# Sample attention of a hybrid decoder step: high and low parts as stationary columns, and four steps moved

## What is computed

```
h = RMSNorm(x);  z = h @ w_in          # 544 rows, one combined projection
A: mLSTM, 4 heads;  B: dilated sliding-window attention, 6 heads;  C: block-sparse attention, 6 heads
y = sum_b sigmoid(gate_b) * (branch_b @ w_br_b);  x = x + y @ w_out;  x = x + SwiGLU(RMSNorm(x))
def dsa_group_sample(q, k, v, buf, bias_tab, win, dil):      # B for the samples
    kv = concatenate([buf, stack([k, v])])                   # window buffer of 128 or 256 cached positions
    s = einsum('bthd,btjhd->bthj', q, g[:, :, :, 0]) * Dh ** -0.5 + bias
    p, lse = softmax_lse(s);  o = einsum('bthj,btjhd->bthd', p, g[:, :, :, 1])
```

## Time and profile before

| | |
|---|---|
| median of 3 runs | 998.3 us (997.5 to 999.62) |
| the profiled execution | 997.17 us |
| its span, first to last instruction | 995.4 us |
| TensorE matmul busy | 972.5 us, 98% |
| VectorE busy | 487.0 us, 49% |
| ScalarE busy | 337.5 us, 34% |
| granted TensorE clock, mean | 0.998 of full |

### The profile page before, as it was taken

One profiled execution on the slowest core, in us unless ns is written; L12 is line 12 of the kernel. 1 busy time (PEld: TensorE's weight loads), 2 busy tenths in 40 slices (PEclk: granted clock), 3 DMA queues, 4 the chain that ended last, 5 costly groups with the idle time before them and its releaser, 6 DMA issues.

```text
span 995.4 us, 18277 instructions
## 1 busy us (share of the span) xinstructions
PE 972.5 (98%) x7624; PEld 947.2 (95%) x7624; DVE 487.0 (49%) x886; ACT 337.5 (34%) x577; POOL 75.6 (8%) x106
## 2 busy tenths in 40 slices
PE   6999999999999999999999999999999999999998
PEld 5899989999889899999999999999999999999997
DVE  5735566444886122645355565555445555323232
ACT  7443233444553441322222342222222222222122
POOL 0100022011301100111113000000000000000000
PEclk9999999999999999999999999999999999999999
DMA  7586437322321764222222222222223222222302
GB/s 251 149 251 235 76 90 152 114 81 78 103 60 35 224 196 114 84 86 86 85 86 85 86 85 86 85 86 88 94 96 98 94 85 75 86 74 76 116 2 90
DMA packets 104909, 105.03 MB, mean 106 GB/s; under 512 B 11130, under 2 KB 101752, under 8 KB 104492
## 3 DMA queue, kind: packets, MB, share of 16 engines
q1 hardware_dynamic: 101224, 92.78, 30.3%
q0 software_dynamic: 3552, 11.08, 3.6%
q10 hardware_dynamic: 52, 0.01, 0.0%
HBM read 98.00 MB, written 15.45 MB: 114 GB/s over the span
## 4 chain that ended last, share of the span: by engine, by line
PE 89%; DVE 5%; issue 1%; ACT 1%; POOL 1%; SPq 1%; DMA 1%; ACTq 0%; DVEq 0%; POOLq 0%
PE acc L451 75%; PE acc L1108 2%; PE acc L1057 1%; PE acc L1033 1%; PE acc L1144 1%; POOL mt L830 1%; DVE w_lo L435 1%; PE acc L1091 1%; PE acc L911 1%; PE acc L900 1%; SPq L681 1%; PE acc L871 1%; PE acc L1017 1%; DVE h_lo L2069 1%; PE acc L1232 1%
## 5 line engine op out<-in xcount | busy, mean ns | idle before, releaser
L451 PE MATMUL acc<-h_hi,w_hi 128*128 128x256 f32 (+1 forms) x1520 | 465.1, 306 | 2.1 <-DVE w_lo L435 1.6
L451 PE MATMUL acc<-h_lo,w_hi 128*128 128x256 f32 (+1 forms) x1520 | 437.7, 288 | 0.0
L451 PE MATMUL acc<-h_hi,w_lo 128*128 128x256 f32 (+1 forms) x1520 | 435.8, 287 | 0.0
L451 PEld LDWEIGHTS acc<-h_hi,w_hi 128*128 128x128 f32 x1520 | 285.8, 188 | 10.3 <-issue 4.2
L430 ACT ACTIVATE w_hi<-raw 128x1024 fp32r<-128x1024 f32 x135 | 141.4, 1047 | 441.7 <-PE acc L451 441.6
L451 PEld LDWEIGHTS acc<-h_lo,w_hi 128*128 128x128 f32 x1520 | 286.1, 188 | 4.8 <-issue 2.4
L451 PEld LDWEIGHTS acc<-h_hi,w_lo 128*128 128x128 f32 x1520 | 286.1, 188 | 0.0
L435 DVE TENSOR_TENSOR w_lo<-raw,w_hi 128x1024 fp32r<-128x1024 f32 x135 | 165.3, 1225 | 112.5 <-ACT w_hi L430 107.8
L451 PE MATMUL acc<-s_hi,w_hi 128*128 128x256 f32 (+1 forms) x352 | 101.6, 288 | 0.0
L451 PE MATMUL acc<-s_lo,w_hi 128*128 128x256 f32 (+1 forms) x352 | 101.3, 288 | 0.0
L451 PE MATMUL acc<-s_hi,w_lo 128*128 128x256 f32 (+1 forms) x352 | 100.7, 286 | 0.0
(11 more groups left out here) (334 smaller groups left out, 1116.9 us busy)
## 6 DMA issues: line engine op xcount, KB each, us to landing
raw<-in_w_in SPq DMA_DIRECT2D x25, 1024.0 KB, 5.1
raw<-in_w_gate_up SPq DMA_DIRECT2D x22, 1024.0 KB, 4.9
raw<-in_w_down SPq DMA_DIRECT2D x8, 1024.0 KB, 4.8
rev<-tab POOLq DMA_DIRECT2D x1, 4352.0 KB, 19.1
ring<-in_cache_dsa_kv SPq DMA_DIRECT2D x4, 1024.0 KB, 6.7
raw<-in_w_out SPq DMA_DIRECT2D x4, 1024.0 KB, 4.7
out<-in_cache_dsa_kv SPq DMA_DIRECT2D x2, 2016.0 KB
ring<-in_cache_moba_k SPq DMA_DIRECT2D x48, 64.0 KB, 2.1
```

The lines of the kernel that those rows point to most:

```text
L451: ins = nc.tensor.matmul(acc[:, bank, 0:HALF[half]], a[:, k, :], two(b[:, kx + k, :], half), start=first and k == k0 and c == 0, stop=last ...
```

## The change

1. **Sample attention, keys.** `Qpad` is fp32r: columns 0 to 63 of a sample hold the high part of the queries, columns 64 to 127 the low part. The transposed keys are split: ScalarE writes the high part of four tiles (512 columns) into `KTs[n % 2]`, VectorE the low part. 22 steps take the place of 48. For each sample there are two fp32r passes (keys high, keys low) with the same stationary operand, in place of one fp32 matmul. The results of the high and the low queries stand in different partitions; ScalarE copies the other half (`low_s`) and VectorE adds (`sums`, three times).
2. **Values.** The same: `V_hi` (ScalarE, 1024 columns, two buffers) and `V_lo` (VectorE, in place of the ring's data) for each of the 11 steps, two fp32r passes of 128 columns for each sample; the new tokens' part comes last; the output is copied in two pieces, transposed in six tiles, and high and low are added (L2059's place).
3. **Block 0** has 64 high and 64 low columns in one stationary operand, and two passes in place of three.
4. **Moved:** `split_hi(0)` and `split_lo(0)` ahead of x's; ScalarE's exp and log of the mLSTM behind `split_hi(3)`; `factors` by a quarter of a block; the cache copies to blocks 66, 70 and 74; the end: sums of squares of the first seven slices and the first transposes ahead of the wait for the last slice. Due times of the sample attention are new.

```diff
-        Qpad = m("Qpad", [P, 2, NB, P])
+        Qpad = m("Qpad", [P, 2, NB, P], F32R)
...
-        KTs = Map(a_s + 8192, 2048)("KTs", [P, 2, 256])
+        V_hi = [Map(a_a + 9216, 4096)("V_hi0", [P, NB, P], F32R), Map(sq_at, 4096)("V_hi1", [P, NB, P], F32R)]
...
+        KTs = [Map(a_a + 9216, 4096)("KTs0", [P, 2, 512], F32R), Map(sq_at, 4096)("KTs1", [P, 2, 512], F32R)]
...
-        loads.append(([(0, 0, rows(w_in, 0, KD, 1024, 32)), (0, 32, rows(w_in, 0, KD, 1028, 96))], P))
+        loads.append(([(0, 0, rows(w_in, 0, KD, 1024, 32)), (0, 32, rows(w_in, 0, KD, 1028, 32))], P))
...
+                passes = ((hi, x_hi), (hi, x_lo)) if w == 0 else ((hi, x_hi), (hi, x_lo), (lo, x_hi))
...
-        T_SA, T_F = 33, 29.1
-        T_QK, D_QK = 1.3, 0.042
-        T_SM, T_P, D_PV = 3.4, 4.6, 0.05
+        T_SA, T_F = 33, 29.35
+        T_QK, D_QK = 1.3, 0.075
+        T_SM, T_P, D_PV = 2.95, 4.05, 0.11
...
+        k_steps = [(m, range(b, b + 4 // NC4[q])) for m, q in enumerate(Q_ORDER) for b in range(0, NB, 4 // NC4[q])]
+        k_ends = [max(n for n, step in enumerate(k_steps) if step[0] == m) + 1 for m in range(6)]
+        K_BANK = (2, 6, 7)
...
-                    when = (0.4, 0.41, 0.42, 0.43, 1.7, 2.05, 2.35, 2.7, 3.05, 3.4, 4.8, 4.9)
+                    when = (0.4, 0.41, 0.42, 0.43, 1.7, 2.05, 2.35, 2.7, 3.0, 3.05, 4.45, 4.5)
...
-                                sp.wait_ge(sem("kt_tr"), NB * (n - 3))
+                                sp.wait_ge(sem("kt_tr"), k_ends[n - 4])
...
                     turn_k(0)
-                    for n in range(6 * NB):
-                        m, b = divmod(n, NB)
+                    turn_k(1)
+                    for n, (m, batches) in enumerate(k_steps):
                         q = Q_ORDER[m]
                         yield T_SA + T_QK + n * D_QK
-                        if n + 1 < 6 * NB:
-                            turn_k(n + 1)
+                        if n + 2 < len(k_steps):
+                            turn_k(n + 2)
                         pe.wait_ge(sem("kt_ev"), n + 1)
...
-                        nc.tensor.matmul(acc[:, 3 + q % 3, 2 * P - w:2 * P], Qpad[:, q // 3, b, :], KTs[:, n % 2, 0:w],
...
+                        for i, b in enumerate(batches):
+                            for c in range(2):
+                                ins = nc.tensor.matmul(scores4(q)[:, 2 * P - w:2 * P], Qpad[:, m % 2, b, :], KTs[n % 2][:, c, w * i:w * (i + 1)],
...
+                            for n, V in enumerate((V_hi[j % 2], v_tiles(V_lo, q, c))):
+                                ins = nc.tensor.matmul(out4(q), Qpad[:, j % 2, b, :], V[:, b, :],
...
                 pe.wait_ge(sem("ssq3_done"), KD - 1)
+                for i in range(NT + 1):
+                    n = out_rows(i)
+                    nc.tensor.matmul(acc[0:n, 7, i:i + 1], ssq[:, P * i:P * i + n], ones[:, 0:1], start=i == 0, stop=False,
+                                     skip_group_check=True)
+                pe.wait_ge(acc_ev, n_sum - 2)
+                pe.wait_ge(sem("xg_done"), KD - 1)
+                y_turned(0, range(4))
+                pe.wait_ge(sem("sq3_done"), KD)
...
-                    yield 1.4
+                    yield 2.1
                     act.wait_ge(sem("f_ready"), 1)
...
+                        nc.scalar.copy(KTs[n % 2][:, 0, :], acc[:, K_BANK[n % 3], :]).then_inc(sem("kt_hi"), 1)
...
+                        nc.scalar.copy(low_s[0:HD, g, c:2 * P], scores4(g)[HD:P, c:2 * P]).then_inc(sem("low_ev"), 1)
+                        nc.scalar.copy(low_s[HD:P, g, :], scores4(3 + g)[0:HD]).then_inc(sem("low_ev"), 1)
...
+                        yield T_SA + (T_SM + 0.3 + 0.2 * j if j < 2 else T_P + 0.06 + (j - 0.9) * D_PV)
+                        tiles, done, count = ring_tiles("v", q)
+                        act.wait_ge(done, count)
+                        act.wait_ge(sem("qk4"), len(k_steps))
+                        if j >= 2:
+                            act.wait_ge(sem("pv_mm"), j - 1)
+                        nc.scalar.copy(V_hi[j % 2][:, :, :], v_tiles(ring, q, c)).then_inc(sem("v_hi"), 1)
...
+                split_hi(act, 0)
                 x_hi(0)
...
-                split_hi(act, 0)
                 squares(1), squares(2)
...
+                        nc.vector.tensor_tensor(KTs[n % 2][:, 1, :], acc[:, K_BANK[n % 3], :], KTs[n % 2][:, 0, :].bitcast(F32),
+                                                ALU.subtract).then_inc(sem("kt_ev"), 1)
...
+                        nc.vector.tensor_tensor(v_tiles(V_lo, q, c), v_tiles(ring, q, c), V_hi[j % 2][:, :, :].bitcast(F32),
+                                                ALU.subtract).then_inc(sem("v_lo"), 1)
...
+                split_lo(dve, 0)
                 x_lo(0)
...
-                split_lo(dve, 0)
```

More of the change, by code:

```diff
@@ L449, in products @@
                     part(half, kx + k)
-                for c, (a, b) in enumerate(((hi, x_hi), (hi, x_lo), (lo, x_hi))):
+                passes = ((hi, x_hi), (hi, x_lo)) if w == 0 else ((hi, x_hi), (hi, x_lo), (lo, x_hi))
+                for c, (a, b) in enumerate(passes):
                     ins = nc.tensor.matmul(acc[:, bank, 0:HALF[half]], a[:, k, :], two(b[:, kx + k, :], half),
                                            start=first and k == k0 and c == 0,
-                                           stop=last and k == k1 - 1 and c == 2)
+                                           stop=last and k == k1 - 1 and c == len(passes) - 1)
                 if k == k1 - 1:
@@ L1127, in sample_outputs, with out4 @@
                     ins.then_inc(sem("pt4"), 1)
-                    yield T_SA + T_P + 0.05
-                    pe.wait_ge(sem("ptn_ev"), 1)
-                    pe.wait_ge(sem("kt_ev"), 6 * NB)
-                    for q in range(6):
-                        half, g = divmod(q, 3)
-                        nc.tensor.matmul(acc[HD * half:HD * (half + 1), 7, P * g:P * (g + 1)], PTn[:, g, HD * half:HD * (half + 1)],
-                                         vn[:, P * q:P * (q + 1)], start=g == 0, stop=False, skip_group_check=True)
+                    pe.wait_ge(sem("kt_ev"), len(k_steps))
+                    def out4(q):
+                        return acc[:, 7 - q // 4, P * (q % 4):P * (q % 4 + 1)]
                     for j, (q, c) in enumerate(pv):
-                        tiles, done, count = ring_tiles("v", q)
-                        half, g = divmod(q, 3)
                         for b in range(NB):
@@ L1224, in _, with out_rows, y_turned @@
[L1224 to L1227 removed]
+                def out_rows(i):
+                    return P if i < NT else TS
+                def y_turned(i, ks):
+                    n = out_rows(i)
+                    for k in ks:
+                        ins = nc.tensor.transpose(acc[0:n, y_bank(i) + k // 4, P * (k % 4):P * (k % 4 + 1)],
+                                                  xT[:, k, P * i:P * i + n], ident)
+                    return ins
@@ new lines, in _ @@
+                for i in range(NT + 1):
+                    n = out_rows(i)
+                    ins = nc.tensor.matmul(acc[0:n, 7, i:i + 1], sq[:, (KD - 1) % 2, P * i:P * i + n], ones[:, 0:1],
+                                           start=False, stop=True, skip_group_check=True)
+                ins.then_inc(sem("rt_mm"), 1)
+                y_turned(0, range(4, KD - 1))
+                pe.wait_ge(sem("xg_done"), KD)
+                y_turned(0, range(KD - 1, KD)).then_inc(sem("y_tr"), 1)
@@ L1228, in _ @@
+                pe.wait_ge(acc_ev, n_sum)
+                for i in range(1, NT + 1):
                     if i >= 3:
@@ L1425, in sample @@
                 def sample():
-                    for n in range(6 * NB):
-                        yield T_SA + T_QK + (n - 0.5) * D_QK
+                    yield T_SA + 0.75
+                    act.wait_ge(sem("new_mm"), 1)
+                    nc.scalar.copy(new_s[:, :, :], acc[:, 2, 0:3 * TS].rearrange("p (g n) -> p g n", n=TS)).then_inc(sem("new_ev"), 1)
+                    for n in range(len(k_steps)):
+                        yield T_SA + T_QK + (n - 1.8) * D_QK
                         act.wait_ge(sem("kt_tr"), n + 1)
@@ new lines, in sums @@
+                def sums(g):
+                    dve.wait_ge(sem("low_ev"), 2 * g + 2)
+                    if g == 0:
+                        dve.wait_ge(sem("mask_in"), 16 * HEADS)
+                        dve.wait_ge(sem("pool_set"), SET["s4"])
+                    c = P if g == 0 else 0
+                    first, second = S4[0:HD, g, c:2 * P], S4[HD:P, g, 0:2 * P]
+                    v.do(nc.vector.tensor_tensor(first, scores4(g)[0:HD, c:2 * P], first, ALU.add))
+                    v.then(nc.vector.tensor_tensor(second, scores4(3 + g)[HD:P], second, ALU.add))
+                    if g == 0:
+                        v.do(nc.vector.tensor_tensor(first, low_s[0:HD, g, c:2 * P], first, ALU.add))
+                        v.then(nc.vector.tensor_tensor(second, low_s[HD:P, g, :], second, ALU.add))
```

(10 more changed lines are left out.)

166 lines of the change are left out of this document (100 added, 66 removed).

## The result

The changed kernel takes 1005.84 us (median of 4 runs, 1004.91 to 1007.29) beside 998.22 us for the kernel before in the same session (997.5 to 999.62); the ratio is 1.0073, 95% interval 1.0051 to 1.0095. The profiled execution is 1005.18 us, its span 1003.3 us, where the kernel before has 997.17 and 995.4. I had predicted 994.6, with 1000.0 as the upper end.

A forecast was written before the change was run, and what follows sets the result against it. The prediction took TensorE's stream (98% busy) as the bound. Its terms summed to -3.7 us, from the profiled 997.2 to 993.5, or 994.6 as a median 1.1 above it; the range was 987 to 1000.

The forecast's parts named there:

- Rival E: TensorE drops to half clock after page waits in the keys; three such stretches, +2.5 us, 997; chance 7%.
- Values, +1.0: Sample attention's values: narrow passes at 0.111 us gain TensorE nothing, late pages and disturbed splits cost 1.0 us.
- A: Rival for the values: narrow passes stream at 0.058 to 0.08 us, 4 of 9 us arrive, 990.6; chance 20%.
- D: Rival for the values: a narrow fp32r pass costs 0.225 us, as much as the fp32 matmul it halves, 1014.5; chance 10%.
- Keys, -4.0: Sample attention's keys: TensorE's work falls 7.8 us, but late pages hold it back; keys end at 363.4, gaining 4.0 us.
- B: Rival for the keys: the pages aren't late, up to 4.5 us more gained, 990; chance 12%.
- C: Rival: ScalarE's and VectorE's copies bound, collisions with weight splits after 356 us reach TensorE, +4.5 us, 999; chance 13%.
- Softmax, +3.0: Between keys and values: the softmax chain grows to 9.9 us against 6.9 before TensorE asks for it, costing 3.0 us.
- Behind the values, +1.3: After the values: second output copy, three more transposes, two more VectorE operations, block 39 starting nearer; costing 1.3 us.
- Start, -2.0: Start and block 0: earlier split gains 1.1 us, moving ScalarE's exp and log removes TensorE waits, 0.9 us.
- Factors, -1.0: Factors moved a quarter block away from the weight split: half of TensorE's 1.93 us loss there, 1.0 us, gained.
- End, -2.0: End of the kernel: five of ten sums and most first transposes go ahead of the last slice, gaining 2.0 us.

The follow-up runs named there:

- end_order: Kernel before with the reordered end and only the start's order (block 0's splits first, exp and log later; block 0 keeps three passes): 994.65 us, ratio 0.9950.
- end_start: Kernel before with the reordered end and the whole change of the start, block 0 in two passes: 997.21 us, ratio 0.9990.
- last_fp32: Changed kernel with the matmuls of value steps 8 to 10 in fp32 on the high part alone: 1000.96 us.
- fill9: Changed kernel with 9 extra unused fp32r matmuls of 256 columns ahead of the wait for value step 8: 998.4 us, ratio 1.0001.
- keys_end_order: Kernel before with changed keys (values fp32), moved cache copies, reordered end and the start's order (block 0 keeps three passes): 993.27 us, ratio 0.9943.

## Why the prediction was wrong

The miss is 11.2 us. Half clock behind the values' wait is 7.3 of it, a term that the forecast had at nothing. By its own steps:

- **Rival E** was the mechanism, with the wrong place, size and chance. I wrote of half clock "a microsecond at half clock costs half" and "three such stretches, the first hidden by the pages: +2.5", for the keys' waits, with 7%. It never asked it of the values, where the same text had a wait growing from 1.13 to some 2.1 us with narrow passes around it. The wait came as worked out (2.04), the half clock behind it lasted 20.5 us and cost 7.3. The step that failed is this pricing: half clock was asked only of the keys, and a stretch was priced as a few microseconds, for which no row gave a length. The runs show that it lasts as long as the work behind the wait leaves the clock down.
- **Values, +1.0.** Narrow passes are 0.11 us apart: A and D are out, and the one-column row was the right guide. The wait and the late pages came as worked out. Of the term's own content little is wrong; what it lacked is the 7.3 above.
- **Keys, -4.0.** The keys end at 362.9 (forecast 363.4), key passes are 0.118 apart, the pages are late where they were said to be (B is out), though the wait at 331.64 us, for q = 3, is 1.10 where 3.6 was forecast:

```profile
PE acc L1119 <- DMA ring<-in_cache_moba_k: 2.4, 2, 1.6
PE acc L1119 <- DMA ring<-in_cache_dsa_kv: 2.2, 2, 1.2
PE acc L1172 <- DVE V_lo L2165: 2.0, 1, 2.0
PE acc L1154 <- DVE S L2141: 1.7, 1, 1.7
PE acc L1139 <- DVE KTs L2104: 0.5, 3, 0.2
```

  (columns: who waits for what, us in total, times, longest). TensorE's wait for the copies of the keys is 0.5 us in all: C is out for the keys. One reading of the forecast was off: its phase of 44.8 us less 12.1 and 28.7 leaves 4.0 us of small waits, where it says some 3; that enters only the outer end of the term.
- **Softmax, +3.0.** 1.68 for `p4` and 0.77 for `Qpad`, 0.87 at a block's sums: 3.3. Right. The value splits stand in it as said (0.95 and 1.23 us at 369.1 and 370.1 us).
- **Behind the values, +1.3.** From the end of the values and new tokens to block 39's second half it is 8.2 us before (404.60 to 412.78) and 9.3 in the kernel with fp32 values at full clock (401.67 to 410.95): +1.1. Right.
- **Start, -2.0.** The mechanism was right for the order (end_order: -1.6 by its trace) and wrong for block 0: "nothing more", I wrote of its passes, and did not cost the two extra operations of `evac` for each half, in front of the split for block 2. They make a wait of 1.54 us, and in some executions a drop of the clock behind it. Net -0.8 in the changed kernel's profile, and no gain in end_start's median.
- **Factors, -1.0.** +0.5 by the landmarks at 46 and 319 us in the changed kernel, +0.2 by the same landmarks alone. The products moved ahead of the landing of their own DMA; I priced the split they avoid, not what they wait for.
- **Cache copies, 0.** No ScalarE or TensorE wait on weights appears; right as far as the trace shows.
- **End, -2.0.** -1.9 in the profile, -2.2 alone. Right, within the range given.

With the terms as measured: start -0.8, factors +0.5, keys to block 39 +10.1 (7.3 clock, 2.8 the rest against 1.3 forecast), end -1.9: +7.9 of span, as seen. So the half clock is the largest part of the miss and not all of it: without it the changed kernel would be near 998.5, no faster than the kernel before, because the start gained 1.2 less than forecast, the factors 1.5 less, and the stretch from the keys to block 39 cost 1.5 more. That last 1.5 has no single step in the traces.

The Trainium skill (TensorE: Matmul & The Clock Gate, HAM oscillation — how this bites in real kernels) describes waits for data of about 3 to 5 us, after each of which the next tile begins at half rate. The half clock behind waits here agrees with that, but a wait of 2.04 us was enough for it in the changed kernel, so on the length the measurement decides. The same page (The HAM clock gate) ties the clock to how busy TensorE is; here its records are busy for 19.99 of 20 us at 0.50, so for narrow fp32r passes the measurement decides against reading "busy" off the profile's busy time.

## What to carry to other kernels

A wait of TensorE has two prices: its length, and half clock for as long as the work behind it doesn't bring the clock back. Look at what stands behind each wait of 1.5 us or more that a change makes: fp32 matmuls of the same size brought it back here, a stream of narrow fp32r passes did not. A few useless passes in a wait can be cheaper than the wait, and splitting fp32 work into fp32r passes gains TensorE nothing when the passes are 128 columns wide: two of them cost 0.21 to 0.22 us here, as much as the fp32 matmul that they replace.

## What the runs showed that I had not expected

- Half clock lasted 20.5 and 23.9 us with TensorE busy all the time, and 9 extra passes of no use (1.06 us) took the time from 1005.8 to 998.4.
- The same kernel can have the drop in one execution and not in another: the kernel with fp32 values ran 993.67 at a mean clock of 0.999 and 1001.11 at 0.992. Waits of 1.5 us (the start) are followed by a drop in some profiled executions (end_start, last_fp32) and not in others (the changed kernel, fill9). Two waits close together can do it too: 1.06 and 1.59 us at block 39 in keys_end_order.
- A narrow fp32r pass of 128 columns is 0.11 us from the next, one of 256 columns 0.118.
